# Low parts of the late expert scores moved from VectorE to POOL, and a number row read from PSUM

## The chip, the cores and the metric

The kernel runs on one core of one Trainium2 chip. The metric is the device time of one execution in microseconds. The core has the engines TensorE (PE, with its weight loads PEld), VectorE (DVE), ScalarE (ACT) and GpSimd (POOL), and the queues that issue DMAs (SP, ACT and POOL).

## The reference, cut to what matters

One trunk layer is computed for 128 context and 512 latent tokens of 1024 features: a mixer, then PEER, an expert retrieval over 16384 experts, and a final norm. The part that the change touches is PEER:

```python
def block(args):                      # 128 tokens; eb: 8 heads x 16 chosen experts, gbk: their softmax weights
    xb, eb, gbk = args
    ub = jnp.take(u_tab, eb, axis=0)
    act = jax.nn.gelu(jnp.einsum('cd,ced->ce', xb, ub))
    vb = jnp.take(v_tab, eb, axis=0)
    return jnp.einsum('ce,ced->cd', gbk * act, vb)
```

## The kernel before

PEER is done in two ways at once. For the 128 context tokens and the first 32 latent tokens (`KS`) the chosen rows of `u_tab` and `v_tab` are gathered by indirect DMAs, 128 rows of 4 KB each, and multiplied on VectorE: one gather and one dot product (`dots`) for each of `NG` = 160 places. For the other 480 latent tokens (`TD`) nothing is gathered. All 16384 experts are worked through in `NE` = 128 blocks of 128: `expert_scores` multiplies a block of `u` with the tokens on TensorE, ACT takes the gelu of it (`gelu_out`) and writes it to DRAM (240 KB), and in the value stage it comes back, is multiplied by a gate that is zero for experts not chosen, and TensorE multiplies it with the block of `v_tab`.

Every product of float32 data is done in three matmuls of a shorter format. The raw block `raw` is copied to a high part `wHi` on ACT (`w_hi`), and the low part is `wLo = raw - wHi`, a subtraction over 128x1024. PE then multiplies high by high, high by low and low by high: 24 matmuls of 480 columns for a block. `wHi` and `wLo` have two buffers, `raw` four. The subtraction releases `raw_used`, for which both PE's `expert_scores` and SP's next load of that `raw` buffer wait. ACT makes `wHi` of block n+2 when PE is done with block n.

The score blocks fall into two stages. In the first `U1` = 68 blocks POOL makes the low parts and issues the gathers of the first `D1` = 80 places between them, while VectorE searches the top experts. In the last `U2` = 60 blocks, which are the late scores, TensorE also makes the gates: after each block's scores `gates_of` multiplies one-hots of the two key numbers of eight tokens, in two halves `q` of four tokens each. VectorE makes the one-hots (`one_hots`): for each half one `tensor_tensor` compares a row of numbers 0 to 127 (`iota128`) with the four tokens' second keys and writes `ohB` (128x512), and four `tensor_scalar` compare the same row with the first key and multiply by the weight, into `ohA` (128x128 each). A half may be overwritten when ACT has copied the products of the half before from PSUM to `stage` (`bank_free`). Every eight blocks ACT writes a `stage` buffer to `gate_scratch` (4 MB) on the queue that also carries the gelu writes; this happens six times.

VectorE's order in a block of this stage is: one-hots of both halves, one or two dots (four in three blocks), the low part of the block after next (`low`, line 1631). The two first low parts stand between the six last dots of the stage before. The first 48 of the 80 dots here multiply by `htokP`, the tokens' row in PSUM, the last 32 by `htok2` in SBUF. POOL in this stage only copies indices and issues gathers (line 496). It waits at each for `row_free`, a count of dots done, so that it stays eight dots ahead (four from place 144 on). Every engine works strictly in its own program's order.

ACT fills some rows in PSUM once, before the first block: `htokP` and `iotaP`, then `psum_in` tells VectorE that they are there.

Of the kernel before, what the change touches and what calls it, by code (L numbers as in the profile page):

```python
# [30 lines left out]
D1 = 80  # L31
# [121 lines left out]
def build(nc, xT, posT, cT, vecs_d, iota_d, invc_d, gw_d, pw_d, keys_d, wblk, ublk, u_tab, v_tab, ident_d, iota128_d, gel_d, gate_d, yT, st_out):  # L153
# [139 lines left out]
    htokP = P[2][:, :, :].rearrange("p a n -> p (a n)")  # L293
    iotaP, i1P = P[3][:, 1, 0:16], P[3][:, 1, 16:16 + SLOTS].rearrange("p (a c) -> p a c", a=2)

    def row(n):

        return rows[:, n, :] if n < VR else rowsX[:, n - VR, :]
# [159 lines left out]
    @block.gpsimd  # L458
    def _(pool):
        def high_of(name, m):  # L460
            g, n = G[name, m], POS[name, m]
            pool.wait_ge(raw_ld[n % RAW], n // RAW * 16 + 16)
            pool.tensor_copy(wHi[:, g % 2, :], raw[:, n % RAW, :]).then_inc(s["hi_first"], 1)

        def low_of(name, m):
            g, r, kk = G[name, m], POS[name, m] % RAW, 512 if name == "upp" else D
            if g < 2:
                pool.wait_ge(s["hi_first"], g + 1)
            else:
                pool.wait_ge(s["w_hi"], g + 1)  # L470
            if (name, m) == ("wq", 1):
                pool.wait_ge(s["sq_used"], 2 * KC)
            pool.tensor_tensor(wLo[:, g % 2, 0:kk], raw[:, r, 0:kk], wHi[:, g % 2, 0:kk].bitcast(f32),  # L473
                               ALU.subtract).then_inc(raw_used[r], 1)

        def low(i, per, n):

            pool.wait_ge(s["w_hi"], i * per + (P_U + n + 1))
            pool.tensor_tensor(wLo[:, n % 2, :], raw[:, n % 4, :], wHi[:, n % 2, :].bitcast(f32),  # L479
                               ALU.subtract).then_inc(raw_used[n % 4], 1)  # L480

        pool.wait_ge(s["sq_used"], KC)
        for name, m in products():
            if G[name, m] < 2:
                high_of(name, m)
            low_of(name, m)
        def indices(i, per, col, buf, at, n, count, last=True):

            pool.tensor_copy(Eg[:, buf, at:at + n], E[:, ds(col, n)]).then_inc(s["eg_ready"], 1)
            if last:  # L490
                hold(pool, s["eg_ready"], i * per + count, s["pool_held"])

        def gather(i, per, free, n, buf, at, tab):

            hold(pool, s["row_free"], i * per + free, s["pool_held"])
            pool.indirect_dma_start(out=row(n), out_offset=None, in_=tab,  # L496
                                    in_offset=bass.IndirectOffsetOnAxis(ap=Eg[:, buf, at:at + 1], axis=0)
                                    ).then_inc(row_ld[n], 16)

        for b in range(8):  # L500
            low(0, 0, b)
        pool.wait_ge(s["x_pk"], 16)
        pool.wait_ge(s["e_ready"], 1)
        pool.wait_ge(s["row_free"], UR)
        with pool.Fori(0, D1 // 16) as i:
            for b in range(12):
                low(i, 12, 8 + b)
                for g in range(b * 4 // 3, (b + 1) * 4 // 3):
                    if g % 8 == 0:
                        indices(i, 2, i * 16 + g, g // 8, 0, 8, g // 8 + 1)  # L510
                    gather(i, 16, g + 1, g % UR, g // 8, g % 8, u_tab)
        with pool.Fori(0, (SLOTS - D1) // 16) as i:
            for g in range(16):
                if g % 8 == 0:
                    indices(i, 2, i * 16 + (D1 + g), g // 8, 0, 8, (D1 + g) // 8 + 1)
                gather(i, 16, D1 + g + 1, g % UR, g // 8, g % 8, u_tab)
        pool.wait_ge(s["e_ready"], 2)
        for seq in range(SLOTS, NG):
            if seq % 8 == 0:
                indices(0, 0, seq, seq // 8 % 2, 0, 8, seq // 8 + 1)  # L520
            if seq < NG - 16:
                gather(0, 0, seq + 1, seq % UR, seq // 8 % 2, seq % 8, u_tab)
            else:
                gather(0, 0, seq + UR - VR + 1, seq % VR, seq // 8 % 2, seq % 8, u_tab)
        with pool.Fori(0, NE // 16) as i:
            for half in range(2):
                indices(i, 4, i * 16 + half * 8, half, 0, 8, 0, last=False)
                indices(i, 4, i * 4 + (SLOTS + half * 2), half, 8, 2, NG // 8 + half * 2 + 2)
                for g in range(8):
                    v = half * 10 + g + g // 4  # L530
                    gather(i, 20, NG + UR - VR + v + 1, v % VR, half, g, v_tab)
                    if g % 4 == 3:
                        gather(i, 20, NG + UR - VR + v + 2, (v + 1) % VR, half, 8 + g // 4, v_tab)
        for k in (0, 2):
            pool.wait_ge(s["sq_done"], 2 * KC + k + 2)
            pool.tensor_tensor(hs[:, k, C0:T], hs[:, k, C0:T], hs[:, k + 1, C0:T], ALU.add).then_inc(s["pairs_ready"], 1)
# [325 lines left out]
    def _(act):  # L862
# [255 lines left out]
            s_out(j)  # L1118
        act.wait_ge(s["S_ready"], 16)
        actf(htokP, htok[:, :], ACT.Copy)  # L1120
        actf(iotaP, iota16[:, :], ACT.Copy).then_inc(s["psum_in"], 1)

        def gelu_out(i, n0, j):
# [85 lines left out]
    def _(dve):  # L1209
# [421 lines left out]
            V.tensor_tensor(wLo[:, n % 2, :], raw[:, n % 4, :], wHi[:, n % 2, :].bitcast(f32), ALU.subtract  # L1631
                            ).then_inc(raw_used[n % 4], 1)

        def one_hots(i, vec, final=False):
            for b in range(12):
                for q in range(2):
                    dve.wait_ge(s["bank_free"], i * 24 + (b * 2 + q + 1))
                    c = i * 96 + (C0 + b * 8 + q * 4)
                    V.tensor_tensor(ohB[:, q, :, :], iota128[:, :].unsqueeze(1).broadcast_to([128, 4, 128]),
                                    keysel[:, 1:2, ds(c, 4)].rearrange("p a n -> p (a n)").unsqueeze(2).broadcast_to(  # L1640
                                        [128, 4, 128]), ALU.is_equal)
                    for n in range(4):
                        last = V.tensor_scalar(ohA[:, q, n, :], iota128[:, :],
                                               keysel[:, 0:1, ds(c + n, 1)].rearrange("p a n -> p (a n)"),
                                               SC[:, ds(c + n, 1)], ALU.is_equal, ALU.mult)
                    last.then_inc(s["oh_ready"], 1)
                for g in range(b * 4 // 3, (b + 1) * 4 // 3):
                    dots(i, 16, D1 + g, vec)
                if not (final and b >= 10):
                    low(i, 12, P_U + U1, b + 2)  # L1650

        dotted[1] = D1
        early_dots(4)
        low(0, 0, P_U + U1, 0)
        early_dots(2)
        low(0, 0, P_U + U1, 1)
        with dve.Fori(0, (SLOTS - D1) // 16) as i:
            one_hots(i, htokP)
        one_hots(3, htok2[:, :])
        one_hots(4, htok2[:, :], final=True)  # L1660
        dve.wait_ge(s["row_free"], NG + UR)
        dve.sem_inc(s["act_ready"], 1)
        dve.wait_ge(s["bank_free"], 2 + 2 * U2)
# [173 lines left out]
```

## Time and profile before

| | |
|---|---|
| median of 3 runs | 2189.85 us (2189.37 to 2190.43) |
| profiled execution, its own time | 2194.28 us |
| its span, first to last instruction | 2192.5 us |
| mean granted TensorE clock | 0.979 of full speed |
| busy: PE, VectorE, ACT, POOL | 96%, 74%, 36%, 33% |
| stage of the late scores | about 1060 to 1502 us |

All times in the rows are microseconds from the start of the span, unless marked ns. A line of the timeline gives start, duration, engine, line, operation, output and inputs, and in brackets how long the engine had been idle and what released it. "issue" stands for time in which nothing that the profile shows was waited for. `x4` behind a line means that four instructions are merged. The granted clock is a share of 2.4 GHz.

### The profile page before, as it was taken

The numbers are of one execution on the slowest core, as the hardware profiler recorded it, in microseconds if no ns is written. First come the engines' busy times: TensorE is split into PE (matmuls) and PEld (weight loads), VectorE is DVE, ScalarE is ACT, GpSimd is POOL, SyncE is SP. The second block draws the span as 40 slices with busy tenths as digits, with TensorE's granted clock in tenths as the row PEclk, the third lists the DMA queues.
The fourth block names the chain that finished last, engine by engine and source line by source line (L and its number), as shares of the span: only waits on it lengthen the run. The fifth ranks groups of instructions, "written<-read, shape, count | busy, mean of one in ns | idle before, by whom it ended". The sixth has DMA issues, their size and how long they took to land.

```text
span 2192.5 us, 34766 instructions
## 1 busy us (share of the span) xinstructions
PE 2111.8 (96%) x11708; PEld 1879.1 (86%) x11708; DVE 1630.6 (74%) x3336; ACT 799.9 (36%) x1046; POOL 725.6 (33%) x524
## 2 busy tenths in 40 slices
PE   6889998999999999999999999999999999999998
PEld 2889998998899888778888889888888888888887
DVE  4539998242589599993788888887777777777787
ACT  2435555222423322222454445553232323232322
POOL 1223232323133666667422122121222322332331
PEclk8899999999899999999999999999999999999998
DMA  9211222434412688878877677677989989889893
GB/s 368 96 54 58 68 63 68 183 126 169 168 59 78 216 283 279 260 243 284 289 285 285 248 272 292 227 279 245 320 302 313 312 309 367 307 310 317 305 339 115
DMA packets 167482, 502.10 MB, mean 229 GB/s; under 512 B 16608, under 2 KB 74336, under 8 KB 165600
## 3 DMA queue, kind: packets, MB, share of 16 engines
q1 hardware_dynamic: 101872, 273.96, 36.5%
q0 software_dynamic: 46080, 167.79, 22.2%
q10 hardware_dynamic: 19440, 59.25, 6.8%
q8 instruction: 43, 0.70, 0.1%
q14 instruction: 47, 0.39, 0.1%
HBM read 436.45 MB, written 64.50 MB: 228 GB/s over the span
## 4 chain that ended last, share of the span: by engine, by line
PE 78%; DVE 13%; DMA 3%; issue 3%; ACT 2%; SPq 1%; POOL 0%; ACTq 0%; DVEq 0%; POOLq 0%
PE P L840 30%; PE P L557 22%; PE P L751 17%; PE P L775 4%; DMA gel_scratch<-gel 2%; PE P L654 1%; DVE rows L1524 1%; DVE rowsX L1524 1%; PE P L580 1%; DVE oh L1555 1%; DVE oh L1562 1%; DVE keysel L1566 1%; PE P L716 1%; PE P L612 1%; DMA modraw<-in_wblk 1%
## 5 line engine op out<-in xcount | busy, mean ns | idle before, releaser
L864 ACT ACTIVATE wHi<-raw 128x1024 fp32r<-128x1024 f32 x330 | 346.3, 1049 | 1219.9 <-PE P L840 459.4
L751 PE MATMUL P<-hHi,wHi 128*128 128x480 f32 x1024 | 396.1, 387 | 10.8 <-POOL wLo L479 8.1
L751 PE MATMUL P<-hLo,wHi 128*128 128x480 f32 x1024 | 389.3, 380 | 0.0
L751 PE MATMUL P<-hHi,wLo 128*128 128x480 f32 x1024 | 389.1, 380 | 0.0
L1631 DVE TENSOR_TENSOR wLo<-raw,wHi 128x1024 fp32r<-128x1024 f32 x188 | 230.2, 1225 | 167.0 <-ACT wHi L864 162.6
L473 POOL TENSOR_TENSOR wLo<-raw,wHi 128x1024 fp32r<-128x1024 f32 (+1 forms) x76 | 185.2, 2437 | 453.9 <-ACT wHi L864 446.6
L496 POOL DMA_INDIRECT rows<-in_v_tab,Eg x160 | 175.2, 1095 | 468.6 <-DVE accB L1679 225.4
L557 PE MATMUL P<-hHi,wHi 128*128 128x320 f32 x960 | 229.1, 320 | 18.9 <-DVE hLo L1216 14.0
L751 PEld LDWEIGHTS P<-hHi,wHi 128*128 128x128 f32 x1024 | 193.5, 189 | 43.8 <-issue 15.8
L557 PE MATMUL P<-hLo,wHi 128*128 128x320 f32 x960 | 221.1, 311 | 0.0
L557 PE MATMUL P<-hHi,wLo 128*128 128x320 f32 x960 | 220.8, 311 | 0.0
L751 PEld LDWEIGHTS P<-hHi,wLo 128*128 128x128 f32 x1024 | 193.0, 189 | 30.2
L751 PEld LDWEIGHTS P<-hLo,wHi 128*128 128x128 f32 x1024 | 193.5, 189 | 28.2
L840 PE MATMUL P<-wfHib,wLo 128*128 128x480 f32 x512 | 195.0, 381 | 0.0
L840 PE MATMUL P<-wfLob,wHi 128*128 128x480 f32 x512 | 194.9, 381 | 0.0
L840 PE MATMUL P<-wfHia,wHi 128*128 128x480 f32 x512 | 194.2, 379 | 0.0
L840 PE MATMUL P<-wfHib,wHi 128*128 128x480 f32 x512 | 194.1, 379 | 0.0
L840 PE MATMUL P<-wfHia,wLo 128*128 128x480 f32 x512 | 193.5, 378 | 0.0
L840 PE MATMUL P<-wfLoa,wHi 128*128 128x480 f32 x512 | 192.3, 376 | 0.0
L479 POOL TENSOR_TENSOR wLo<-raw,wHi 128x1024 fp32r<-128x1024 f32 x68 | 163.5, 2404 | 79.7 <-ACT wHi L864 79.3
L557 PEld LDWEIGHTS P<-hHi,wHi 128*128 128x128 f32 x960 | 162.9, 191 | 25.4 <-issue 16.5
L496 POOL DMA_INDIRECT rows<-in_u_tab,Eg x88 | 94.8, 1077 | 235.8 <-DVE rows L1524 169.9
(250 smaller groups left out, 3761.2 us busy)
## 6 DMA issues: line engine op xcount, KB each, us to landing
raw<-in_ublk SPq DMA_DIRECT2D x128, 512.0 KB
raw<-in_v_tab SPq DMA_DIRECT2D x128, 512.0 KB
raw<-in_wblk SPq DMA_DIRECT2D x104, 512.0 KB
gel_scratch<-gel ACTq DMA_DIRECT2D x128, 240.0 KB
gsr<-gel_scratch SPq DMA_DIRECT2D x128, 240.0 KB
gate_scratch<-stage ACTq DMA_DIRECT2D x6, 4096.0 KB
gates4a<-gate_scratch SPq DMA_DIRECT2D x16, 768.0 KB
gates4b<-gate_scratch SPq DMA_DIRECT2D x16, 768.0 KB
```

Of the source, the lines that this page charges most:

```text
L473: pool.tensor_tensor(wLo[:, g % 2, 0:kk], raw[:, r, 0:kk], wHi[:, g % 2, 0:kk].bitcast(f32), ALU.subtract).then_inc(raw_used[r], 1)
L479: pool.tensor_tensor(wLo[:, n % 2, :], raw[:, n % 4, :], wHi[:, n % 2, :].bitcast(f32), ALU.subtract).then_inc(raw_used[n % 4], 1)
L496: pool.indirect_dma_start(out=row(n), out_offset=None, in_=tab, in_offset=bass.IndirectOffsetOnAxis(ap=Eg[:, buf, at:at + 1], axis=0)).the ...
L557: last = nc.tensor.matmul(P[g % 2][:, h, 0:HALF], w_[:, g % 2, k * 128:(k + 1) * 128], cols(x_, k, h), start=(st and a == 0 and b == 0), s ...
L580: last = nc.tensor.matmul(parts_of(m)[32 * j:32 * j + 32, :], c32[:, k, :], raw[:, n % RAW, k * 128:(k + 1) * 128], start=(a == 0), stop=( ...
L612: last = nc.tensor.matmul(P[r // 4][0:2, r // 2 % 2, r % 2 * 256:r % 2 * 256 + 256] .rearrange("p (a n) -> p a n", a=2), cvec[:, 2 * k:2 * ...
L751: last = nc.tensor.matmul(P[0][:, j % 2, 0:TD], w_[:, j % 2, k * 128:(k + 1) * 128], x_[:, k, C0:T], start=(k == 0 and a == 0 and b == 0), ...
L775: last = nc.tensor.matmul(P[1][:, q, n * 128:(n + 1) * 128], ohB[:, q, n, :], ohA[:, q, n, :], start=True, stop=True)
L840: last = nc.tensor.matmul(P[k // 2][:, k % 2, 0:TD], w_[:, j % 2, k * 128:(k + 1) * 128], x_[j % 2][:, :], start=(first and a == 0 and b = ...
L864: return nc.scalar.activation(out, in_, f, **kw)
L1524: V.scalar_tensor_tensor(out=row(b), in0=row(b), scalar=1.0, in1=vec, op0=ALU.mult, op1=ALU.mult, accum_out=actv[:, ds(i * per + n, 1)]).t ...
L1631: V.tensor_tensor(wLo[:, n % 2, :], raw[:, n % 4, :], wHi[:, n % 2, :].bitcast(f32), ALU.subtract).then_inc(raw_used[n % 4], 1)
```

## The change

POOL's two loops of gathers in the late stage become one loop over the 60 blocks, written out: first the low part of the block, then its one or two gathers, with the index copies where they fall. POOL's own `low` is the helper of the first stage. VectorE's `one_hots` no longer calls `low`, and the six dots ahead of the stage are done in a row. A second row of numbers, `iota128P`, is placed in PSUM by ACT, and the comparison for `ohB` reads it there. The four comparisons for `ohA` still read `iota128` in SBUF. VectorE's `low` stays for the value stage.

```diff
+    iota128P = P[3][:, 1, 16 + SLOTS:144 + SLOTS]
...
-        with pool.Fori(0, (SLOTS - D1) // 16) as i:
-            for g in range(16):
-                if g % 8 == 0:
-                    indices(i, 2, i * 16 + (D1 + g), g // 8, 0, 8, (D1 + g) // 8 + 1)
-                gather(i, 16, D1 + g + 1, g % UR, g // 8, g % 8, u_tab)
-        pool.wait_ge(s["e_ready"], 2)
-        for seq in range(SLOTS, NG):
-            if seq % 8 == 0:
-                indices(0, 0, seq, seq // 8 % 2, 0, 8, seq // 8 + 1)
-            if seq < NG - 16:
-                gather(0, 0, seq + 1, seq % UR, seq // 8 % 2, seq % 8, u_tab)
-            else:
-                gather(0, 0, seq + UR - VR + 1, seq % VR, seq // 8 % 2, seq % 8, u_tab)
+        for b in range(U2):
+            low(0, 0, U1 + b)
+            for seq in range(D1 + b * (NG - D1) // U2, D1 + (b + 1) * (NG - D1) // U2):
+                if seq == SLOTS:
+                    pool.wait_ge(s["e_ready"], 2)
+                if seq % 8 == 0:
+                    indices(0, 0, seq, seq // 8 % 2, 0, 8, seq // 8 + 1)
+                if seq < NG - 16:
+                    gather(0, 0, seq + 1, seq % UR, seq // 8 % 2, seq % 8, u_tab)
+                else:
+                    gather(0, 0, seq + UR - VR + 1, seq % VR, seq // 8 % 2, seq % 8, u_tab)
...
         actf(htokP, htok[:, :], ACT.Copy)
+        actf(iota128P, iota128[:, :], ACT.Copy)
         actf(iotaP, iota16[:, :], ACT.Copy).then_inc(s["psum_in"], 1)
...
-        def one_hots(i, vec, final=False):
+        def one_hots(i, vec):
...
-                    V.tensor_tensor(ohB[:, q, :, :], iota128[:, :].unsqueeze(1).broadcast_to([128, 4, 128]),
+                    V.tensor_tensor(ohB[:, q, :, :], iota128P.unsqueeze(1).broadcast_to([128, 4, 128]),
...
-                if not (final and b >= 10):
-                    low(i, 12, P_U + U1, b + 2)
...
-        early_dots(4)
-        low(0, 0, P_U + U1, 0)
-        early_dots(2)
-        low(0, 0, P_U + U1, 1)
+        early_dots(6)
```

## Rows read from the trace of the kernel before

**Rows 1.** the page, part 1: busy us, share of span, instructions
```profile
PE 2111.8 (96%) x11708; PEld 1879.1 (86%) x11708; DVE 1630.6 (74%) x3336; ACT 799.9 (36%) x1046; POOL 725.6 (33%) x524
```

**Rows 2.** waits of PE, 1060 to 1502: us, times, longest
```profile
PE P L775 <- DVE ohA L1643: 8.6, 7, 3.1
```

**Rows 3.** timeline 1040 to 1110: start, us, engine, line [idle before]
```profile
1061.51 1.22 DVE L1524 SCALAR_TENSOR_TENSOR rows<-rows,P 128x1024 f32<-128x1024 f32 x1
...
1064.84 1.06 ACT L864 ACTIVATE wHi<-raw 128x1024 fp32r<-128x1024 f32 x1 [4.99 <-issue]
...
1066.08 1.22 DVE L1631 TENSOR_TENSOR wLo<-raw,wHi 128x1024 fp32r<-128x1024 f32 x1
...
1067.43 0.76 PE L751 MATMUL P<-hHi,wHi 128*128 128x480 f32 x1 [2.69 <-issue]
...
1070.63 0.68 DVE L1639 TENSOR_TENSOR ohB<-iota,keysel 128x512 f32<-128x512 f32 x1
...
1072.87 1.10 DVE L1643 TENSOR_SCALAR ohA<-iota,keysel,SC 128x128 f32<-128x128 f32 x4
```

**Rows 4.** one stretch: PE PEld DVE ACT POOL, granted clock, DMA share
```profile
1067.00:1071.00 4.00, 3.57 (x9) 3.01 (x10) 4.00 (x7) 0.00 (x0) 2.39 (x3) 0.57 0.98 342
```

**Rows 5.** chain that ended last, 1040 to 1110: start, us, what
```profile
1067.43 7.01 PE P L751 x24
...
1074.44 1.78 PE P L775 x16
...
1076.23 5.22 PE P L751 x24
```

**Rows 6.** timeline of ACT and VectorE in a regular block, 1290 to 1345
```profile
1298.40 1.06 ACT L864 ACTIVATE wHi<-raw 128x1024 fp32r<-128x1024 f32 x1 [2.74 <-PE P L751]
...
1301.87 0.69 DVE L1639 TENSOR_TENSOR ohB<-iota,keysel 128x512 f32<-128x512 f32 x1 [1.15 <-ACT stage L864]
```

**Rows 7.** timeline of ACT and POOL in the scores before, 1040 to 1110
```profile
1047.93 1.06 ACT L864 ACTIVATE wHi<-raw 128x1024 fp32r<-128x1024 f32 x1 [1.03 <-PE P L751]
...
1049.07 2.40 POOL L479 TENSOR_TENSOR wLo<-raw,wHi 128x1024 fp32r<-128x1024 f32 x1 [1.76 <-ACT wHi L864]
```

**Rows 8.** timeline of POOL and VectorE, the first gather and its dot
```profile
738.09 1.12 POOL L496 DMA_INDIRECT rows<-in_u_tab,Eg  x1 [1.14 <-issue]
...
743.83 1.22 DVE L1524 SCALAR_TENSOR_TENSOR rows<-rows,P 128x1024 f32<-128x1024 f32 x1 [20.77 <-DMA rows<-in_u_tab,Eg]
```

**Rows 9.** chain that ended last, 1195 to 1222: start, us, what
```profile
1188.24 16.49 DMA gel_scratch<-gel
...
1209.52 1.12 DVE ohA L1643 x4
```

**Rows 10.** timeline of POOL and VectorE, 436 to 482
```profile
438.95 2.81 POOL L473 TENSOR_TENSOR wLo<-raw,wHi 128x1024 fp32r<-128x1024 f32 x1 [5.10 <-ACT wHi L864]
...
439.42 3.02 DVE L1425 TENSOR_TENSOR hLo<-hs,hHi 128x640 fp32r<-128x640 f32 x1
...
471.14 0.82 DVE L1425 TENSOR_TENSOR hLo<-hs,hHi 128x640 fp32r<-128x640 f32 x1
```

**Rows 11.** two lines of VectorE: duration ns min/median/max, first and last start
```profile
L1357 DVE TENSOR_SCALAR xc<-xrp,vecs x8: 608/610/2070, 137.8 to 330.7; 128x644 f32<-128x644 f32 x8
...
L1643 DVE TENSOR_SCALAR ohA<-iota,keysel,SC x480: 331/341/444, 1071.2 to 1494.8; 128x128 f32<-128x128 f32 x160
```

**Rows 12.** timeline of ACT behind a gate store, 1184 to 1226
```profile
1204.75 0.57 ACT L864 ACTIVATE gel<-P 128x480 f32<-128x480 f32 x1 [3.17 <-DMA gel_scratch<-gel]
...
1207.82 1.05 ACT L864 ACTIVATE wHi<-raw 128x1024 fp32r<-128x1024 f32 x1
```

**Rows 13.** timeline of PE: its waits behind two more gate stores
```profile
1269.41 1.16 PE L775 MATMUL P<-ohA,ohB 128*128 128x128 f32 x8 [1.80 <-DVE ohA L1643]
...
1438.81 1.16 PE L775 MATMUL P<-ohA,ohB 128*128 128x128 f32 x8 [0.72 <-DVE ohA L1643]
```

More of the change, by code:

```diff
@@ L1659, in _ @@
         one_hots(3, htok2[:, :])
-        one_hots(4, htok2[:, :], final=True)
+        one_hots(4, htok2[:, :])
         dve.wait_ge(s["row_free"], NG + UR)
```

## The prediction

> **What bounds the kernel now.** I read the page first: TensorE is busy for 96% of the span and VectorE for 74% [rows 1]. So time can only be won where PE waits, and lost where something new makes it wait. The change touches one stage, the 60 late expert scores (1060 to 1502 us). There the list of waits of PE has one large entry: 8.6 us in 7 waits for `ohA`, the one-hots of the gate products [rows 2]. The low parts `wLo` do not appear under their own name, but the timeline shows one wait that belongs to them: block 68's first matmul starts at 1067.43 after 2.69 us of idleness, put down to "issue" [rows 3]. VectorE began that block's low part only at 1066.08, behind four dots and two copies, and it lasts 1.22 us: it ends at 1067.3 [rows 3]. The row blames nobody; the times do.
>
> After that wait the granted clock is 0.57 of full speed, the lower of the two levels (1.2 GHz) for most of the four us after [rows 4], and the 24 matmuls of the block take 7.01 us where those of the next block take 5.22 [rows 5]. The wait thus costs 2.69 + 1.79 = 4.5 us. A regular block is 5.22 us of scores and 1.78 of gate products, 7.0 us [rows 5].
>
> In a regular block VectorE is not late. ACT starts the high part of block b+2 at 1298.40, when block b's scores are done; VectorE starts the next one-hots 3.47 us later, and what it waited for last is ACT's copy of the gate products, not its own work [rows 6]. Taking 1.14 us of subtraction out of its queue moves nothing there.
>
> **The change, part by part.** *Low part on POOL, regular blocks.* In the loop before, POOL starts a low part 1.14 us after ACT starts the high part (1047.93 to 1049.07) and needs 2.40 us for it, twice VectorE's 1.22 [rows 7]. In block time, with ACT's high part at 0, it would run from 1.1 to 3.5 us. PE wants it at 7.0 + 1.8 = 8.8 us: 5 us of cover, so 0 in the sum. If that cover were gone each block would pay 1.2 us more than now. The raw buffer is freed about 1.3 us later, and its next load has three more blocks, over 20 us, before ACT reads it: 0.
>
> *Gathers behind the low parts.* POOL is in order, so the gathers of block b+2 now stand behind `low(b+2)`, and that waits for ACT's high part. Today a gather runs eight dots ahead, some six blocks. Then it is issued at about 3.7 us of block b's time, and its dot comes at about 6.8 us of block b+1's, 10 us later. A gather alone took 5.74 us from issue to its dot (738.09 to 743.83) [rows 8]: covered, 0. Under the 4 MB gate store, which is issued every eighth block, no row gives a gather's landing; the nearest one is a 240 KB write queued behind such a store, 16.49 us [rows 9]. That is the upper end, 6.5 us too late for one dot, of which some 2.5 us are slack (the dots end at about 0.9 us of block time, the one-hots start at 3.5); the lower end is 0. Between them I take 0, as several blocks pass before the next store and most landings should be nearer to the 5.74 us; the range keeps 1 to 4 us a store. An index copy before every eighth gather and the register work stay as they are.
>
> *The number row from PSUM.* `ohB` reads one of its two inputs from PSUM. The dots have that form already, and stand at 1.22 us beside POOL [rows 3]: duration unchanged, 0. ACT's extra copy of 128 columns is once, some 0.2 us beside PE's block: 0.
>
> *What POOL's long subtraction does to VectorE.* This is the term that decides. Two rows show that VectorE and POOL exclude each other for some instructions. POOL asks for its subtraction at 438.95 and needs 2.81 us; VectorE, busy with another instruction until then, issues its next at 439.42, and that takes 3.02 us, where the same takes 0.82 at 471.14 [rows 10]. So POOL, waiting, gets in at the boundary, and the VectorE instruction waits for all of POOL's 2.3 us. The second row is the form of `ohA`: a tensor_scalar with two pointer scalars and input and output in SBUF. At 644 elements it takes 0.61 us, but up to 2.07 [rows 11]; `ohA` with 128 elements takes 0.34, so 0.27 us for 516 elements, 0.52 ns each [rows 11], less than half of the 1.19 ns of the low part (1.22 us for 1024) [rows 3]. It is a fast form, and one that gets blocked. The change moves only `ohB` to PSUM; the four `ohA` of each half keep `iota128` in SBUF. The Trainium skill says the same (SBUF — State Buffer, Who interferes with whom): the shared port pair goes to whoever issues first, for the whole instruction, and `tensor_scalar` in SBUF is among the forms that take it. The trace agrees, with 2.07 against 0.61 us. By this rule the next two terms are due; were `ohA` free of it, the sum would be the gain of the first block alone, -3.6 us.
>
> In a regular block the two miss each other: POOL is done at 3.5 us, the first `ohA` starts at 4.1. They meet where VectorE is late, at two kinds of place.
>
> *The first block.* POOL does `low(68)` right after ACT's high part, so PE starts block 68 at about 1064.8 and the 4.5 us go. Scores then end at 1070.0. VectorE's six dots, now in one row, end at 1061.51 + 6 x 1.14 = 1068.35, the two halves of one-hots 1.7 and 3.34 us later (1070.63 to 1073.97 in the rows) [rows 3]: 1070.05 and 1071.7. But at 1070.06 ACT starts the high part of block 70, and POOL's subtraction asks at 1071.2, while the last `ohA` would start at about 1071.4. If POOL gets in, the second half is ready at 1074.1, PE idles 3 us, the clock drops again (1.8 us), and scores of block 69 start at 1074.1 + 0.9 + 1.8 = 1076.8, against 1076.23 now: +0.5. If POOL comes 0.2 us later, they start at 1072.6: -3.6. By the start times I take the first.
>
> *The blocks after a gate store.* The gelu write of one block sits behind the 4 MB store for 16.49 us and ACT waits for it until 1204.75 [rows 9, 12]; its stage copies, then the one-hots, come 3 us late. ACT goes from the copies straight to the next high part at 1207.82 [rows 12], so POOL's subtraction would ask at 1208.96 and run to 1211.3, right over the second half's `ohA` at 1209.52 [rows 9]. They would end at 1212.4 where they end at 1210.6: +1.8 us of PE. The same shape stands at 1269.41 and 1438.81, where PE already waits 1.80 and 0.72 us [rows 13]. Each costs between these 1.8 us and POOL's whole 2.4; I take 1.8 and 2.4. Together +6.0. The waits at these two places grow to 3 us or so, near the 2.69 us after which the clock dropped: between 0 and 2 x 1.79 = 3.6 us; I take 1.1, as either wait is made of two pieces with work between.
>
> **Sum.** +0.5 + 6.0 + 1.1 = +7.6 us. The profiled execution took 2194.28 us with a span of 2192.5; the median of the runs is 2189.85. The same 7.6 us on each gives a span near 2200 and a median of 2197.5 us.
>
> **The rivals.**
>
> *It does what it says: faster.* POOL's subtraction misses `ohA` in the first block, and the gelu writes land in time after most stores (the order of gathers, loads and stores shifts by some us, and three of six stores pass without a wait of PE today). Then -3.6, and -4.4 to -10 if one or two of the three stalls (0.7 to 3.8 us each with what follows them) go as well: 2180 to 2185 us. For it: the wait for `wLo` at 1067.43 is real. Against it: nothing in the change speeds the gelu write, and the raw load and the gather of a block now both start just ahead of the store. 20%.
>
> *It moves nothing that can be measured.* The first block wins 3.6 us and the late one-hots pay it back, or one stall less pays for two longer ones: 2185.5 to 2194, middle 2190. 25%. That `ohA` is not blocked at all belongs here too: then only the 3.6 us of gain are left, 2186. Against it: the maximum of 2.07 us [rows 11].
>
> *Late gathers on top.* Gathers issued with the store land 3 to 6 us late, the dots delay the one-hots, which then meet POOL's next subtraction at every store: six times 2.3 + 0.9 us and the clock beside the terms above, 2203 to 2212. For it: the lead falls from six blocks to 10 us, against 16.49 at worst. Against it: 2.5 us slack, and dots are not read before the end of the stage. 12%.
>
> *As forecast*, +4.4 to +13, 2194 to 2203: 43%.
>
> A change within 0.2% (4.4 us) is about what a measurement of this kernel cannot tell from none. So faster 0.20, same 0.25, slower 0.55. The likeliest case's own range is 2194 to 2203; the range that holds 8 in 10 goes from 2184 (the gain with one stall less) to 2207 (late gathers at some stores).
>
> **What would show it.** After the change, block 68 starts without the 2.69 us, the chain at 1067 loses its 7.01 us piece; `ohA` gets single instructions of 2 to 2.5 us instead of a maximum of 0.444 [rows 11], one at about 1071 and one behind each late gelu; PE's wait for `ohA` grows from 8.6 to 15 us or more. POOL's low parts in the stage stand at 2.4 us. I am wrong if the maximum of `ohA` stays under 0.5 us, if the stalls at the stores go away or double in number, or if dots show waits for gathers in this stage, which they do not today.

## The result, and the profile after

The changed kernel takes 2226.95 us (median; 2225.25 to 2232.86) against 2189.61 us of the kernel before (2188.36 to 2190.43): ratio 1.0176, 95% interval 1.0162 to 1.0190, or 37 us slower. The forecast was 2197.5 us, with 2207 as the upper end of the range. Slower was right; the size was off by 30 us. The profiled execution after has a span of 2223.4 us, that of before 2192.5. These are 30.9 us apart and not 37, because the profiled execution of before (2194.28 us) was one of its slower ones and that of after (2225.25 us) one of its faster ones.

The page after, part 1, in the form of [rows 1]:

```profile
PE 2124.2 (96%) x11708; PEld 1890.4 (85%) x11708; DVE 1570.8 (71%) x3276; ACT 801.0 (36%) x1047; POOL 855.6 (38%) x584
```

VectorE has 60 us less work, POOL 130 us more. The 60 low parts cost twice as long on POOL, as planned. The shares tell nothing about the loss. The waits of the late stage do (1040 to 1540 us; us in total, times, longest), beside [rows 2]:

```profile
PE P L775 <- DVE ohA L1644: 25.6, 9, 6.3
DVE rowsX L1525 <- DMA rowsX<-in_u_tab,Eg: 24.8, 7, 6.1
...
DVE rows L1525 <- DMA rows<-in_u_tab,Eg: 14.6, 2, 8.0
...
ACT gel L864 <- DMA gel_scratch<-gel: 7.7, 6, 2.4
```

PE's wait for the one-hots went from 8.6 to 25.6 us. The second and third line had no counterpart in this stage before: the dots wait 39.4 us, nine times, for the gathered rows. That was named in the prediction as a sign that it is wrong.

The first block came out as forecast. This is the timeline of it, beside [rows 3]:

```profile
1070.67 3.18 DVE L1644 TENSOR_SCALAR ohA<-iota,keysel,SC 128x128 f32<-128x128 f32 x4
...
1071.17 2.35 POOL L481 TENSOR_TENSOR wLo<-raw,wHi 128x1024 fp32r<-128x1024 f32 x1 [1.63 <-ACT wHi L864]
...
1073.91 2.08 PE L775 MATMUL P<-ohA,ohB 128*128 128x128 f32 x8 [2.55 <-DVE ohA L1644]
...
1081.66 1.06 ACT L864 ACTIVATE wHi<-raw 128x1024 fp32r<-128x1024 f32 x1 [4.47 <-PE P L751]
```

PE no longer waits 2.69 us for the low part, but 2.55 us for four `ohA` that take 3.18 us with POOL's subtraction over them (1.1 us else). ACT's high part of block 71, which is made when the scores of block 69 are done, starts at 1081.66, where it started at 1081.48: the forecast said +0.5, it is +0.2. The longest `ohA` is where it was expected too (duration in ns, minimum, median, maximum; the line of before is in [rows 11]):

```profile
L1644 DVE TENSOR_SCALAR ohA<-iota,keysel,SC x480: 327/340/2449, 1069.0 to 1522.6; 128x128 f32<-128x128 f32 x160
```

Regular blocks take 6.96 to 7.06 us, most of them 6.99, as before. The loss is at the gate stores. The first of them, timeline 1126 to 1160:

```profile
1127.30 0.95 POOL L498 DMA_INDIRECT rowsX<-in_u_tab,Eg  x1
...
1127.92 0.35 ACTq L1177 DMA_DIRECT2D gate_scratch<-stage  x1
...
1143.17 1.22 DVE L1525 SCALAR_TENSOR_TENSOR rowsX<-rowsX,P 128x1024 f32<-128x1024 f32 x1 [5.70 <-DMA rowsX<-in_u_tab,Eg]
...
1144.58 1.06 ACT L864 ACTIVATE wHi<-raw 128x1024 fp32r<-128x1024 f32 x1 [2.74 <-PE P L751]
...
1144.92 3.21 DVE L1644 TENSOR_SCALAR ohA<-iota,keysel,SC 128x128 f32<-128x128 f32 x4
...
1145.71 2.34 POOL L481 TENSOR_TENSOR wLo<-raw,wHi 128x1024 fp32r<-128x1024 f32 x1 [2.24 <-ACT wHi L864]
...
1148.19 3.70 PE L775 MATMUL P<-ohA,ohB 128*128 128x128 f32 x16 [3.65 <-DVE ohA L1644]
...
1157.18 1.06 ACT L864 ACTIVATE wHi<-raw 128x1024 fp32r<-128x1024 f32 x1 [4.06 <-PE P L751]
```

Read it from the top. POOL issues the gather of a `rowsX` buffer 0.6 us before ACT issues the 4 MB store. The dot that reads what this gather brought (counted off, gather by gather and dot by dot, over the stage) starts 15.87 us later, after 5.70 us of waiting on the DMA. Away from the stores the same distance is 9 to 10 us, as forecast, and no dot waits. In the first-gather row of before the same was 5.74 us [rows 8]. The late dot pushes the one-hots behind it past the start of POOL's next subtraction, so `ohA` is blocked as well (3.21 us). PE waits 3.65 us, and its 16 gate matmuls take 3.70 us in place of the 1.78 of [rows 5]. The granted clock is 0.62 on average over the two us behind that wait and 0.53 over the next two, which is mostly the lower level (1.2 of 2.4 GHz). The columns are those of [rows 4]:

```profile
1148.00:1150.00 2.00, 1.81 (x9) 1.75 (x10) 2.00 (x7) 0.00 (x0) 1.09 (x3) 0.62 1.03 406
1150.00:1152.00 2.00, 2.00 (x11) 1.98 (x11) 1.51 (x4) 1.07 (x1) 0.10 (x1) 0.53 0.93 314
```

The step from one high part to the next is 12.60 us here (1144.58 to 1157.18) against 6.99: 5.6 us lost, 3.65 of waiting and 1.9 of clock.

What each store costs above 6.99 us a block, worked out in the same way from the starts of ACT's high parts (six stores, issued at 1127.92 to 1437.79 after the change):

| store | 1 | 2 | 3 | 4 | 5 | 6 | sum |
|---|---|---|---|---|---|---|---|
| before | 0.2 | 4.2 | 2.8 | 0 | 0 | 1.7 | 8.9 |
| after | 5.6 | 7.8 | 6.9 | 0.6 | 9.2 | 6.4 | 36.5 |

The difference is 27.6 us of the 30.9 by which the two profiled spans differ. At store 4 the dot came 3.83 us late and still before POOL's subtraction; `ohA` was not blocked, and only 0.6 us were lost. Four `ohA` took 2.27 to 3.21 us at stores 1, 3 and 6. At store 5, the dearest, it was the late dot itself that the subtraction held. From place 128 on a dot reads both its inputs from SBUF, and this one took 3.33 us in place of 1.22:

```profile
1390.31 2.34 POOL L481 TENSOR_TENSOR wLo<-raw,wHi 128x1024 fp32r<-128x1024 f32 x1 [2.67 <-ACT wHi L864]
...
1390.41 3.33 DVE L1525 SCALAR_TENSOR_TENSOR rowsX<-rowsX,htok 128x1024 f32<-128x1024 f32 x1 [6.12 <-DMA rowsX<-in_u_tab,Eg]
```

### The profile page after: what moved, and what is told of

Read it like the earlier page. It is cut to its first block, busy times and chain, and to the rows that moved or that the text cites. A ratio compares the mean times of both kernels' runs of the same rounds, so it can differ in the third digit from the quotient of the medians.

```text
span 2223.4 us, 34664 instructions
## 1 busy us (share of the span) xinstructions
PE 2124.2 (96%) x11708; PEld 1890.4 (85%) x11708; DVE 1570.8 (71%) x3276; ACT 801.0 (36%) x1047; POOL 855.6 (38%) x584
## 4 chain that ended last, share of the span: by engine, by line
PE 72%; DVE 13%; issue 5%; DMA 4%; POOL 3%; ACT 2%; SPq 1%; DVEq 0%; POOLq 0%; ACTq 0%
PE P L840 30%; PE P L557 21%; PE P L751 13%; PE P L775 3%; POOL wLo L481 2%; DMA rows<-in_u_tab,Eg 2%; DMA rowsX<-in_u_tab,Eg 2%; DVE rowsX L1525 1%; DVE rows L1525 1%; PE P L654 1%; PE P L580 1%; DVE oh L1556 1%; DVE oh L1563 1%; DVE keysel L1567 1%; PE P L716 1%
## 5 line engine op out<-in xcount | busy, mean ns | idle before, releaser
L481 POOL TENSOR_TENSOR wLo<-raw,wHi 128x1024 fp32r<-128x1024 f32 x128 | 310.8, 2428 | 287.0 <-ACT wHi L864 286.7
L1632 DVE TENSOR_TENSOR wLo<-raw,wHi 128x1024 fp32r<-128x1024 f32 x128 | 156.9, 1226 | 157.8 <-ACT wHi L864 156.1
L1640 DVE TENSOR_TENSOR ohB<-P,keysel 128x512 f32<-128x512 f32 x120 | 82.3, 686 | 115.3 <-ACT stage L864 115.3
```

The source lines that it names most:

```text
L1640: V.tensor_tensor(ohB[:, q, :, :], iota128P.unsqueeze(1).broadcast_to([128, 4, 128]), keysel[:, 1:2, ds(c, 4)].rearrange("p a n -> p (a n) ...
```

## The experiments

Two explanations stood against each other. The first: the shortened lead of the gathers, together with the 4 MB store, makes the dots late. The second: POOL's subtractions blocking `ohA` do it, only more often than forecast. A third factor was the gelu write that queues behind the store. None of the kernels leaves out work. The times of the kernel before, run beside them, were 2189.7 to 2190.5 us.

**1. The short lead alone**, on the kernel before.

```diff
-        with pool.Fori(0, (SLOTS - D1) // 16) as i:
...
+        for b in range(U2):
+            if b >= 2:
+                pool.wait_ge(s["bank_free"], 2 * b - 1)
+            for seq in range(D1 + b * (NG - D1) // U2, D1 + (b + 1) * (NG - D1) // U2):
```

> The kernel before, with its low parts still on VectorE; only POOL's gathers are held back, so that the gather of a block is issued at most about one block ahead of its dots, as in the kernel after. Nothing is left out. Theory 1 (the shortened lead of the gathers under the 4 MB gate stores causes the loss): the dots wait for their rows at the gate stores as in the kernel after, 4 to 6 of the 6 stalls grow, and the time is 15 to 30 us over the kernel before, 2205 to 2220 us. Theory 2 (POOL's subtractions blocking the ohA compare cause it): no POOL subtraction stands there, so at most 5 us over, 2190 to 2195 us.

2224.56 us, ratio 1.0159 (1.0140 to 1.0177): +35 us, with every low part of this stage still on VectorE. Its waits, and its first store:

```profile
PE P L774 <- DVE ohA L1642: 29.7, 10, 6.4
DVE rowsX L1523 <- DMA rowsX<-in_u_tab,Eg: 28.6, 6, 6.4
...
DVE rows L1523 <- DMA rows<-in_u_tab,Eg: 13.1, 2, 7.0
```

```profile
1126.66 0.94 POOL L496 DMA_INDIRECT rowsX<-in_u_tab,Eg  x1 [4.53 <-ACT stage L863]
...
1126.80 0.35 ACTq L1175 DMA_DIRECT2D gate_scratch<-stage  x1
...
1142.74 1.22 DVE L1523 SCALAR_TENSOR_TENSOR rowsX<-rowsX,P 128x1024 f32<-128x1024 f32 x1 [6.36 <-DMA rowsX<-in_u_tab,Eg]
```

The same stall, 16.08 us from issue to dot, with no subtraction on POOL near. The second explanation allowed at most 5 us. The short lead is enough to make the loss. (It is a little over the expected 30 us. Here VectorE's own low part stands between the late dot and the one-hots, from 1143.88 to 1145.02 at this store.)

**2. The longer lead given back**, on the kernel after.

```diff
+        issued = D1
...
+            due = D1 + (b - 1) * (NG - D1) // U2
+            upto = due + UR if due + UR <= NG - 16 else max(NG - 16, due + VR)
+            upto = min(upto, D1 + 2 + 3 * b, NG)
+            for seq in range(issued, upto):
...
+            issued = upto
```

> The kernel after, low parts on POOL, but the gathers are issued up to eight dots ahead (four ahead near the end) in place of at most two blocks' worth behind each low part. Nothing is left out. Theory 1: the dots no longer wait for rows at the gate stores and the time falls by most of the 37 us, to 2190 to 2200 us; what is left is the first block's wait and POOL's subtractions over ohA. Theory 2: the subtractions stand where they stood, the time stays near 2220 us.

2202.32 us, ratio 1.0045 (1.0031 to 1.0060): 24.6 us of the 37 are back, and the time is 2 us above the expected range. The dots' waits fall from 39.4 to 1.6 us, PE's from 25.6 to 16.1:

```profile
PE P L780 <- DVE ohA L1649: 16.1, 9, 3.2
...
DVE rows L1530 <- DMA rows<-in_u_tab,Eg: 1.6, 1, 1.6
```

What remains is what the prediction had described: behind a late gelu write (ACT waits for it until 1263.80) POOL's subtraction falls on the second half's `ohA`:

```profile
1267.98 2.35 POOL L481 TENSOR_TENSOR wLo<-raw,wHi 128x1024 fp32r<-128x1024 f32 x1 [2.54 <-ACT wHi L869]
...
1268.55 2.63 DVE L1649 TENSOR_SCALAR ohA<-iota,keysel,SC 128x128 f32<-128x128 f32 x4
```

**3. The blocking of `ohA` taken away**, on the kernel after.

```diff
-                        last = V.tensor_scalar(ohA[:, q, n, :], iota128[:, :],
+                        last = V.tensor_scalar(ohA[:, q, n, :], iota128P,
```

> The kernel after, with the second one-hot compare (ohA) reading its number row from PSUM as ohB does, so that no compare of the blocks can be held by a POOL instruction. Nothing is left out. Theory 1: the first block gains its 3 to 4 us, each stall under a gate store gets at most 2 us shorter, the waits for the rows stay: 2205 to 2220 us. Theory 2: the stalls go with the blocking, 2190 us or less. The longest ohA falls from 2449 ns to under 600 ns either way.

2213.46 us, ratio 1.0107 (1.0082 to 1.0132): 13.5 us are back, and the dots still wait 34.5 us.

```profile
L1644 DVE TENSOR_SCALAR ohA<-P,keysel,SC x480: 392/402/408, 1068.8 to 1515.8; 128x128 f32<-128x128 f32 x160
```

With its input in PSUM no `ohA` is blocked any more (408 ns at most), at 60 ns more for each. The blocking made part of the loss, the smaller one. The 13.5 us are a net figure: with the longer `ohA` the dots with both inputs in SBUF start a little later, now meet POOL's subtraction in regular blocks too, and six of them take 3.1 to 3.4 us in place of 1.22 (1.7 us in a seventh).

**4. Both taken away**, with the whole stores.

> The kernel after with the gathers up to eight dots ahead and the compare ohA reading its number row from PSUM, the gate stores whole; nothing is left out. The longer lead alone gave 2202.3 us. If the 12 us that stay over the kernel before are the subtractions on POOL over the compares, they go with the blocking: 2188 to 2193 us. If the stores' other waits make them: 2197 us or more.

2193.39 us, ratio 1.0016 (1.0007 to 1.0025). So the lead is worth 20 us without the blocking and 25 with it; the blocking 9 us with the long lead and 13.5 with the short one. Together they account for 33.6 of the 37 us. Part of what is left is seen in the trace: eight dots with both inputs in SBUF are held by POOL's subtraction (3.1 to 3.4 us), and four blocks between 1347 and 1422 us take 0.9 to 1.0 us more than 6.99.

**5. The store in eight pieces**, on the kernel after, on the kernel before, and on the short lead of experiment 1.

```diff
+        def store_piece(c, half, n):
+            act.dma_start(gate_in[ds(c, 1), :, n * 1024:(n + 1) * 1024].rearrange("a p m -> (a p) m"),
+                          stage[:, half, n * 16:(n + 1) * 16, :].rearrange("p n t -> p (n t)")).then_inc(gate_st[half], 16)
...
+            for n in range(8):
+                gate_block(t * 4 + (half * 2 + n // 4), n % 4, half, n * 8)
+                if n < 7 and not (isinstance(t, int) and half == 0):
+                    store_piece(t * 2 + (half - 1), 1 - half, n + 1)
...
```

> The kernel after, but each 4 MB gate store is issued as eight stores of 0.5 MB, the first at the end of its half and the others after the following blocks. Nothing is left out. Theory 1 and theory 3 (the small gelu write that queues behind the store): no transfer stands behind 4 MB any more, the stalls at the six gate stores mostly vanish, 2180 to 2192 us. Theory 2: the stores do not matter, the time stays near 2220 us.

> The kernel before with each 4 MB gate store issued as eight stores of 0.5 MB after successive blocks; nothing else, and nothing is left out. It sizes what the store itself costs the kernel before through the small gelu write that queues behind it (about 9 us of stalls at three of its six stores): 2178 to 2184 us if that holds. If the stores cost nothing by themselves: 2189 us.

> The kernel before with POOL's gathers held back as in the first experiment (low parts on VectorE) and the gate stores in eight pieces; nothing is left out. With the whole stores the held-back gathers cost about 35 us, and the pieces with the full lead gave 3.4 us under the kernel before. Theory 1 (the short lead costs only where a gather meets a 4 MB store): as with the full lead and pieces, 2184 to 2190 us. If the short lead itself is too short for ordinary gathers: well above 2190, 2195 to 2220 us.

On the kernel after: 2188.16 us, ratio 0.9993 (0.9983 to 1.0003). On the kernel before: 2186.80 us, 0.9982 (0.9973 to 0.9992). With the short lead: 2186.57 us, 0.9978 (0.9968 to 0.9989). The short lead costs 35 us with whole stores and nothing with pieces. No dot waits for rows in any of the three. In the third:

```profile
PE P L774 <- DVE ohA L1650: 3.5, 2, 3.1
```

How even the DMA load has become is seen in the busy share of the 16 DMA engines in 40 slices of 1060 to 1480 us, first after the change, then with short lead and pieces. The valleys of 2 to 5 between the stores' nines are gone but for one 5 at the start:

```profile
DMA  8635658983567982467983658985659934759936
```

```profile
DMA  7566678888878888879888888887988888988977
```

The second expectation was missed in size. All waits of ACT behind a gelu write (9.5 us of its time, 8.9 us of blocks in the table) are gone from the kernel before, and in the profiled executions the stage, from the high part of block 68 to the one behind the last, is 8.9 us shorter (444.4 to 435.6 us). Yet the median fell by 3.4 us only. Part of the answer is that the profiled execution of before was itself 4.4 us above its median, and its stalls need not be those of a usual execution: in the kernel of experiment 7, whose stores are whole too, the same stalls add up to 4.6 us. How much they cost in the median execution was not measured.

**6. Long lead and pieces, without and with `ohA` from PSUM.**

> The kernel after with the gathers up to eight dots ahead and the gate stores in eight pieces; nothing is left out. With the pieces alone the kernel after came to 2188 us. Theory 1: no gather is late behind pieces of 0.5 MB, so the longer lead adds nothing: 2183 to 2189 us. If some lateness was left behind the pieces, it falls further, to 2178 to 2183 us.

> The kernel after with the three cures together: gathers up to eight dots ahead, the compare ohA from PSUM, the gate stores in eight pieces; nothing is left out. The first block should take 13.8 us for its two steps, as with ohA from PSUM and the short lead, in place of 18.8, so 3 to 5 us under the 2187.9 us without the PSUM row: 2182 to 2185 us, and faster than both kernels.

> The last one without the longer lead: the kernel after with the compare ohA from PSUM and the gate stores in eight pieces; nothing is left out. If no gather is late behind pieces, 2182 to 2186 us, 2 to 4 us under the 2188.2 us with the pieces alone; if the short lead still costs something, 2187 us or more.

2187.88, 2186.71 and 2187.66 us (ratios 0.9988, 0.9987 and 0.9987, their intervals within 0.9977 to 0.9998). The longer lead adds nothing behind pieces, as the first explanation has it. The gain hoped for from the PSUM row did not come, and both of its expectations were missed. The first block's two steps took 13.9 us, in place of 18.9 with the long lead and 17.3 with the short one. But four blocks between 1344 and 1417 us took 7.83 to 7.86 us in place of 6.99, and two others 0.4 to 0.7 us more. In the four it is the dots with both inputs in SBUF that are held, as at store 5 after the change:

```profile
1345.20 2.38 POOL L481 TENSOR_TENSOR wLo<-raw,wHi 128x1024 fp32r<-128x1024 f32 x1 [1.44 <-ACT wHi L869]
...
1345.37 3.29 DVE L1538 SCALAR_TENSOR_TENSOR rowsX<-rowsX,htok 128x1024 f32<-128x1024 f32 x1
```

Seven dots take 3.3 to 3.4 us here. With `ohA` reading SBUF and the same pieces none does: the eight `ohA` of a block take 0.5 us less, and the dots nearest to a subtraction start 0.4 us or more before it, where the held ones start up to 0.2 us behind it. So the median of 2187.66 us, which by its expectation would mean that the short lead still costs something, has another cause; no dot waits for rows in it.

**7. Only the first low parts on POOL.**

```diff
+        low(0, 0, U1)
+        low(0, 0, U1 + 1)
         with pool.Fori(0, (SLOTS - D1) // 16) as i:
...
-        early_dots(4)
-        low(0, 0, P_U + U1, 0)
-        early_dots(2)
-        low(0, 0, P_U + U1, 1)
+        early_dots(6)
```

> The kernel before with only the first two low parts of the stage (those of experts 68 and 69) on POOL, six dots' gathers behind them, and the others on VectorE behind their one-hots as before; the number row of ohB from SBUF as before. Nothing is left out. If the prediction's first-block arithmetic holds (the wait for the late low part goes and no compare is blocked), 3 to 4.5 us under the kernel before, 2185 to 2187 us. If giving a low part to POOL costs anything by itself, 2190 us or more.

> Both of the last two together (the first two low parts on POOL, and the gate stores in eight pieces) on the kernel before; nothing is left out. If the two add up: 12 to 13 us under the kernel before, 2175 to 2179 us, and faster than both kernels. If one eats the other, near 2182 us.

2189.09 us (0.9999, 0.9989 to 1.0009) and 2187.60 us (0.9983, 0.9974 to 0.9992). Both missed. The first:

```profile
1065.34 2.40 POOL L479 TENSOR_TENSOR wLo<-raw,wHi 128x1024 fp32r<-128x1024 f32 x1 [4.10 <-ACT wHi L866]
...
1068.85 0.98 POOL L496 DMA_INDIRECT rows<-in_u_tab,Eg  x1 [0.97 <-POOL Eg L489]
```

```profile
1074.88 1.22 DVE L1526 SCALAR_TENSOR_TENSOR rows<-rows,P 128x1024 f32<-128x1024 f32 x1 [3.71 <-DMA rows<-in_u_tab,Eg]
```

It is the failed step of the prediction in small. The gathers stand behind the second low part, which waits until 1065.34 for ACT; the first gather goes out at 1068.85 and its dot waits 3.71 us.

**8. Why the store holds gathers up.** Experiment 1 with the store cut in other ways: the eight pieces issued together, two pieces of 2 MB four blocks apart, and the same two issued together.

> The first experiment (kernel before, gathers held back) with each gate store cut into the same eight pieces, all issued one behind the other at the end of the half, so that 4 MB still go out at once, in rows of 4 KB in place of 32 KB. Nothing is left out. If the amount under way at once makes the gathers late: the dots still wait, 2210 to 2225 us. If the long rows of the whole store do: about 2187 us, as with the pieces spread over the blocks.

> The first experiment with each gate store in two pieces of 2 MB, four blocks apart. Nothing is left out. A 2 MB piece should hold up a gather half as long as 4 MB: with 15 to 16 us from issue to dot behind 4 MB and 4 to 6 without a store, about 10 us, which is within the lead of 10 us and the slack of 2.5: 2187 to 2195 us. If the hold-up does not shrink with the amount, twelve late gathers in place of six: 2215 us or more.

> The first experiment with the same two pieces of 2 MB as in the halves, but both issued at the end of the half, one behind the other: the same rows of 16 KB and 4 MB under way at once, with two issues on ACT and not eight. Nothing is left out. If the amount under way makes the gathers late: dots wait 5 to 6 us again, 2215 to 2228 us. If the spacing was irrelevant and the shorter rows cured it: 2186 us.

2228.07 us (1.0172, 1.0157 to 1.0188), 2185.83 us (0.9983, 0.9974 to 0.9992) and 2206.77 us (1.0076, 1.0054 to 1.0097). The first is a little over its range, the second a little under.

The eight together are no evidence on the gathers, though the number fits: no dot waits for rows there. ACT itself stalls:

```profile
1127.87 8.99 ACTq L1168 DMA_DIRECT2D gate_scratch<-stage  x8
1136.96 1.06 ACT L863 ACTIVATE wHi<-raw 128x1024 fp32r<-128x1024 f32 x1 [9.12 <-issue]
```

Eight issues take 8.99 us, where one alone takes 0.35, and the next high part is late by that. In the third kernel two issues together take 0.8 to 1.1 us. Halves apart, then halves together, at the first store:

```profile
1126.85 0.94 POOL L496 DMA_INDIRECT rowsX<-in_u_tab,Eg  x1 [4.53 <-ACT stage L863]
```

```profile
1137.09 1.22 DVE L1531 SCALAR_TENSOR_TENSOR rowsX<-rowsX,P 128x1024 f32<-128x1024 f32 x1 [0.56 <-DMA rowsX<-in_u_tab,Eg]
```

```profile
1124.32 0.94 POOL L496 DMA_INDIRECT rowsX<-in_u_tab,Eg  x1 [4.53 <-ACT stage L863]
...
1136.49 1.22 DVE L1527 SCALAR_TENSOR_TENSOR rowsX<-rowsX,P 128x1024 f32<-128x1024 f32 x1 [2.48 <-DMA rowsX<-in_u_tab,Eg]
```

From issue to dot, each ended by the DMA, at the first store: 16.08 us behind 4 MB in rows of 32 KB (experiment 1), 12.17 us behind 4 MB in rows of 16 KB, 10.24 us behind 2 MB in rows of 16 KB. Over all stores the dots that waited came 14.1 to 17.8, 10.9 to 15.9 and 8.7 to 11.0 us after their gathers. So shorter rows helped with the amount unchanged, spacing helped again, and neither of the two expectations of the last run was right alone. Of the 35 us, 18 went with the shorter rows and the rest with the spacing. (Cutting the rows also made two DMAs of one; the runs don't part the two.) The Trainium skill (DMA: Bandwidth & Descriptors, Queues, rings and completion order) says that a DMA engine takes turns between its queues by whole packets. The trace has the store as packets of 32 KB in experiment 1 and of 16 KB in the last run, and those of a gather as 4 KB. That fits: a gather whose turns alternate with packets of 32 KB waits longer for each than with 16 KB. No run here counts the turns, nor shows that the skill's packets are those of the trace, so this stays an explanation that agrees.

**9. A version that beats both.** Only the first low part on POOL, the second on VectorE behind the six dots, with eight pieces, then with two halves apart.

```diff
+        low(0, 0, U1)
         with pool.Fori(0, (SLOTS - D1) // 16) as i:
...
-        early_dots(4)
-        low(0, 0, P_U + U1, 0)
-        early_dots(2)
+        early_dots(6)
         low(0, 0, P_U + U1, 1)
```

> The kernel before with the gate stores in eight pieces and only the first low part (expert 68) on POOL, the second one on VectorE behind the six dots. Nothing is left out. With both on POOL a gather came late behind the second one and the first block gained next to nothing. If that was the cause, the first block now starts without its wait and no dot waits for rows: 2 to 3 us under the 2186.8 us of the pieces alone, 2183.5 to 2185.5 us. If PE's wait only moves to the one-hots behind the second low part: 2186 to 2188 us.

> The best so far (kernel before, only the first low part on POOL, eight pieces: 2184.7 us) with two pieces of 2 MB four blocks apart in place of the eight. Nothing is left out. Two pieces were as good as eight with the gathers held back, so the same within the measurement, 2183 to 2187 us; if 2 MB still hold the gelu writes up, 2187 to 2190 us.

2184.71 us (0.9979, 0.9970 to 0.9988) and 2182.05 us (0.9963, 0.9949 to 0.9976). The second has the lowest median of all, 7.7 us under the kernel before and 45 under the change. That it is faster than the first isn't shown: their intervals overlap, and in the profiled executions their 60 blocks take the same, 420.7 and 420.9 us. In the first, 3.4 of the 5.8 us are those of the pieces alone (experiment 5). In the first of the two PE's wait only moved, from the low part (2.69 us) to the one-hots behind it:

```profile
1071.45 1.16 PE L776 MATMUL P<-ohA,ohB 128*128 128x128 f32 x8 [1.32 <-issue]
1073.17 1.16 PE L776 MATMUL P<-ohA,ohB 128*128 128x128 f32 x8 [0.56 <-DVE ohA L1652]
```

Over the first three steps that is 1.0 us less than before, not the 2 to 3 expected. The second kernel is 1 us under its expected range.

## Why the prediction was wrong

**The step that failed** is "Gathers behind the low parts". It saw the lead fall from eight dots to 10 us, bounded the landing under a gate store between 5.74 and 16.49 us [rows 8, 9], and took 0, "as several blocks pass before the next store and most landings should be nearer to the 5.74 us". The runs put the landing at the upper end: at the first store the dot came 15.87 us after its gather, 16.08 in experiment 1, and 14 to 18 us over all six. The lead itself was forecast well, at 10 us. The argument mistook what had to be covered. It is of no use that seven of eight blocks have no store; each of the six stores is met by a gather that POOL issues within 0.8 us of ACT's issue of the store, because both now hang on the same block. The upper bound, 6.5 us late for one dot, was about right: 5.70 and 6.36 us at the first store, 3.83 to 8.00 over all six. So it was passed in places, and the value taken, 0, was wrong at every store.

**The slack of 2.5 us** was about right, a little more was there: at store 4, with 3.83 us of lateness, 0.6 us were lost. Beyond it lateness turned into PE's wait, and at four of the six stores VectorE also met POOL's subtraction.

**The rival "Late gathers on top"** described the mechanism but was given 12% and 2203 to 2212 us. That range isn't the sum of its own terms. "Six times 2.3 + 0.9 us" on top of 2197.5 is 2216.7, above the range, and with 1.8 us of clock at each store 2227.5, where 2226.95 was measured. So its price for a store was good on average (3.2 us and 1.8 of clock, against 27.6 / 6 = 4.6 us measured in the traces); the range fell short of it. The dots came 4 to 8 us late and not 3 to 6. That the total fits so closely is partly luck: the stores lost from 0.6 to 9.2 us, and "the terms above" already hold 6.0 us for blocking at three of the same stores. Its "for it" already had the row, 16.49 us.

**The first block**: +0.5 forecast, +0.2 measured, and by the mechanism named, with a wait of 2.55 us where 3 were forecast. The scores of block 69 started at 1075.64, 0.6 us earlier than before, and then lost that and more to the clock. The alternative was right in its direction and smaller than said: with `ohA` from PSUM the two steps took 13.8 us in place of 16.6, -2.8 and not -3.6.

**The blocks after a gate store**: the blocking was real, and forecast at +6.0 and 1.1 us of clock. With the lead given back (experiment 2) the kernel has nearly the prediction's terms alone: +10 us by the ratio (7 to 13), where the sum said +7.6, and 2202.3 us lies within the likeliest case's own range. The total is kinder than the parts. The blocking stood at stores 3, 4 and 5, which lost 5.7, 4.6 and 3.4 us. The forecast had it at 2, 3 and 6, and 2 and 6 lost 0.3 and 0.4 us. The first block's two steps took 18.7 us and not 16.6, +2.1 us where +0.5 was forecast. The stalls of all six stores add up to 6.0 us more than before, where 7.1 with the clock was forecast; as their places differ, that this comes so near is partly luck.

**A blocking not foreseen** is that of the dots with both inputs in SBUF, which the prediction did not name. It held one dot after the change (store 5, 9.2 us lost) and took back part of what the PSUM row gained in experiments 3, 4 and 6.

**The low parts in regular blocks and `ohB` from PSUM at 0**: right. Regular blocks stay at 6.96 to 7.06 us, and `ohB` has a median of 687 ns, as before.

**Left open**: how the hold-up divides between amount and row length at other sizes, and why pieces that shorten the stage by 8 to 10 us in the profiled executions, where nearly all low parts are on VectorE, show as 3 to 8 us in the medians. The parts outside the stage differ by up to 6 us between the profiled executions, which is as large as what is to be explained.

## What to carry to other kernels

When prefetches are moved behind other work on an in-order queue, work out the lead that is left in time, and hold it against the slowest landing that any row shows, not the usual one: the largest transfer that starts in the same step as the prefetch decides. If the lead can't be kept, cut that transfer: two pieces of 2 MB some blocks apart made a 35 us loss vanish. Where several terms are bounded from both sides, the one whose upper end repeats at a fixed place of the loop should not be taken at its lower end. And add up a rival's terms before giving its range: here the sum, 2216.7 us and more, would have shown how dear the step taken at 0 could be.

## What the runs showed of the hardware

- A gather of 128 rows of 4 KB, issued within a us of a 4 MB store on another queue, was used 14 to 18 us later by a dot that waited for it (15.9 and 16.1 at the first store), against 5.74 without. At the first store it was 12.2 us with the store in rows of 16 KB in place of 32, and 10.2 us with such rows and half the amount.
- Eight stores of 0.5 MB issued in a row held ACT for 8.99 us; spread over the blocks of experiment 5 most took 0.34 to 0.4 us each, and no regular block of the kernel before lost more than 0.3 us.
- A two-pointer `tensor_scalar` of 128 elements goes from 340 to 402 ns with its input in PSUM, and its maximum from 2449 to 408 ns: no POOL instruction holds it up any more.
- A dot of 1024 elements with both inputs in SBUF took up to 3.4 us when POOL's subtraction had started just before it, against 1.22. The longest of those with the tokens' row in PSUM took 1.2 us beside the same subtraction.
